# Replacing TensorE's spreading of the picks' first halves by a round trip through memory

## The reference

```python
# 8 heads x 16 picks = 128 experts per token, out of 128 x 128 experts;
# expert = 128 * first_half + second_half, each half in 0..127
hid  = hn . down[expert]                # per token and pick: one number
coef = gate * gelu(hid)
h   += sum over picks of coef * up[expert]
out  = rms_norm(h, final_norm_gain)
```

## Time and profile before

| what | value |
|---|---|
| median of 3 runs | 2948.95 us |
| lowest, highest | 2944.47, 2950.55 us |
| the profiled execution's own time | 2950.64 us |
| its span | 2948.8 us |
| TensorE busy | 2814.4 us (95%) |
| VectorE busy | 2062.5 us (70%) |
| ScalarE busy | 1118.8 us (38%) |
| GpSimd busy | 539.3 us (18%) |
| moved | 799.60 MB, 271 GB/s on the mean |

### The profile page before, as it was taken

The page is one execution under the profiler, slowest core; times in us unless marked ns, Lnnn a source line. Parts: engine busy times, 40 slices in busy tenths (PEclk is TensorE's granted clock), DMA queues, the critical chain, the costliest instruction groups (busy, mean ns, idle before and its releaser), DMA issues.

```text
span 2948.8 us, 41367 instructions
## 1 busy us (share of the span) xinstructions
PE 2814.4 (95%) x16385; PEld 2303.8 (78%) x16385; DVE 2062.5 (70%) x3111; ACT 1118.8 (38%) x1741; POOL 539.3 (18%) x534
## 2 busy tenths in 40 slices
PE   6899999999999999999999999999999889999997
PEld 4699999997879988798997798888878777444443
DVE  5687777778775456754655668985568999666666
ACT  3344444445454444544455542012117986000000
POOL 1000000000000000000000002333445457544443
PEclk9999999999999999999999999999999999999999
DMA  9977777777866644365443546999998888999997
GB/s 386 351 261 265 265 267 263 267 266 252 299 207 189 175 124 156 127 200 176 136 123 128 198 140 234 349 331 391 403 366 282 291 295 317 407 409 409 409 410 319
DMA packets 345760, 799.60 MB, mean 271 GB/s; under 512 B 40104, under 2 KB 95648, under 8 KB 344800
## 3 DMA queue, kind: packets, MB, share of 16 engines
q1 hardware_dynamic: 270576, 505.70, 49.6%
q0 software_dynamic: 74992, 291.27, 26.3%
HBM read 794.76 MB, written 2.10 MB: 270 GB/s over the span
## 4 chain that ended last, share of the span: by engine, by line
PE 53%; DMA 22%; DVE 13%; ACT 5%; issue 4%; POOL 3%; SPq 0%; DVEq 0%; ACTq 0%; POOLq 0%
PE ps L2019 16%; PE ps L2021 15%; PE ps L2020 15%; DMA s<-in_up_rows,s 12%; DMA s<-in_down_rows,s 8%; DVE s L1953 4%; POOL s L719 3%; DVE s L1972 2%; ACT s L1163 1%; DMA s<-in_ada_first 1%; DVE r L1246 1%; DMA s<-in_ret_first 1%; ACT r L734 1%; PE ps L2313 1%; ACT s L1133 1%
## 5 line engine op out<-in xcount | busy, mean ns | idle before, releaser
L2019 PE MATMUL ps<-r,r 128*128 128x256 f32 (+1 forms) x3232 | 1043.8, 323 | 9.9 <-DVE r L1246 7.6
L2021 PE MATMUL ps<-r,r 128*128 128x256 f32 (+1 forms) x3232 | 1024.2, 317 | 0.0
L2020 PE MATMUL ps<-r,r 128*128 128x256 f32 (+1 forms) x3232 | 1024.1, 317 | 0.0
L1246 DVE TENSOR_TENSOR r<-s,r 128x1024 fp32r<-128x1024 f32 (+2 forms) x532 | 640.3, 1212 | 413.1 <-ACT r L734 412.1
L734 ACT CAST r<-s 128x1024 fp32r<-128x1024 f32 (+2 forms) x532 | 550.0, 1041 | 766.7 <-PE ps L2021 708.2
L2019 PEld LDWEIGHTS ps<-r,r 128*128 128x128 f32 x3232 | 618.3, 191 | 67.0 <-issue 19.9
L2020 PEld LDWEIGHTS ps<-r,r 128*128 128x128 f32 x3232 | 618.6, 191 | 43.1 <-issue 5.3
L2021 PEld LDWEIGHTS ps<-r,r 128*128 128x128 f32 x3232 | 618.0, 191 | 40.2
L2703 PE MATMUL ps<-s,big 128*128 128x512 f32 x1024 | 441.8, 594 | 2.0 <-DMA s<-in_up_blocks 2.0
L1972 DVE SCALAR_TENSOR_TENSOR s<-s,s,s 128x1024 f32<-128x1024 f32 x256 | 329.2, 1286 | 162.9 <-DMA s<-in_up_rows,s 155.6
L1953 DVE CUSTOM_DVE_ANT_0 s<-s,s 128x1152 f32<-128x1152 f32 x256 | 345.8, 1353 | 111.2 <-DMA s<-in_down_rows,s 110.9
(11 more groups left out here) (314 smaller groups left out, 2240.4 us busy)
## 6 DMA issues: line engine op xcount, KB each, us to landing
s<-in_ada_w SPq DMA_DIRECT2D x128, 512.0 KB, 5.4
s<-in_up_blocks SPq DMA_DIRECT2D x128, 512.0 KB
s<-in_ret_w_in SPq DMA_DIRECT2D x112, 512.0 KB, 5.5
s<-in_down_blocks SPq DMA_DIRECT2D x128, 448.0 KB
s<-in_w_in SPq DMA_DIRECT2D x96, 512.0 KB, 3.9
s<-in_ada_first SPq DMA_DIRECT2D x64, 512.0 KB, 7.9
s<-in_ret_w_out SPq DMA_DIRECT2D x64, 512.0 KB, 5.6
s<-in_ret_w_in SPq DMA_DIRECT2D x112, 256.0 KB, 3.8
```

Source lines behind the costliest of these rows:

```text
L1246: v.tensor_tensor(lo_of(w), raw_of(w), hi_of(w).bitcast(F), ALU.subtract).then_inc(*lo_made.to(w))
L2019: pe.matmul(o, lh, rh, start=start, stop=False, skip_group_check=True)
L2020: pe.matmul(o, lh, rl, start=False, stop=False, skip_group_check=True)
L2021: return pe.matmul(o, ll, rh, start=False, stop=stop, skip_group_check=True)
```

## The change

The first halves of the picks no longer go through TensorE. SyncE stores them to a small tensor in memory (`first_halves`), in eight pieces, once they are chosen. During the picks it loads them back, one load of 256 KB for each group of four tokens, in which one row of 2 KB is repeated over the 128 partitions, into three buffers `FH`. VectorE's `pick` compares these with `POS` and reads the picked rows straight from PSUM, so that ScalarE's copy goes away.

Three things move with it. `FH` lies in the room of the streamed blocks, so SyncE stands in its loop of 64 loads until tile 1's picks are multiplied, and `up`'s blocks 128 and 129 come after that. Four single-use semaphores (`d_fg`, `d_tab`, `d_ff`, `d_f2`) become one, `d_late`. For that, the load of `final_norm_gain_2` is moved from SyncE's queue to GpSimd's: it is issued just before row 326.

```diff
+        FH = [at(W + 6144 + 512 * i, 512) for i in range(3)]
...
-        d_fg, d_tab, d_ff, d_f2, d_step = (dma_sig(n) for n in ("d_fg", "d_tab", "d_ff", "d_f2", "d_step"))
+        d_late, d_step = dma_sig("d_late", ["fg", "tab", "ff", "f2"]), dma_sig("d_step")
...
-        rows_copied = sig("rows_copied", fours)
+        d_kept = dma_sig("d_kept", [(t, k) for t in range(2) for k in range(4)])
+        d_halves = [dma_sig(f"d_halves{i}", [n for n in range(64) if n % 3 == i]) for i in range(3)]
...
             for b in range(256):
+                if b in (50, 82):
+                    t = b // 82
+                    sp.wait_ge(*chosen.at((t, 1)))
+                    for k in range(4):
+                        sp.dma_start(A["halves"][t].rearrange("(q k) m -> k q m", k=4)[k],
+                                     EF[t][32 * k:32 * k + 32, 0, :]).then_inc(*d_kept.to((t, k)))
+                if b == 128:
+                    sp.wait_ge(*d_kept.at((1, 3)))
+                    sp.wait_ge(*block_used.at(127))
+                    for n in range(64):
+                        if n >= 3:
+                            sp.wait_ge(*multiplied.at(fours[n - 3]))
+                        sp.dma_start(FH[n % 3], A["halves"][n // 32].rearrange("(q k) m -> q (k m)", k=4)[n % 32].partition_broadcast(
+                            128)).then_inc(*d_halves[n % 3].to(n))
+                    sp.wait_ge(*multiplied.at((1, 31)))
...
-                if b == 128:
-                    sp.wait_ge(*block_used.at(127))
...
-                if b == 131:
-                    sp.dma_start(G16[0:16, :], A["final_norm_gain_2"].rearrange("(n p) -> n p", p=128)).then_inc(*d_f2.to("all"))
...
                 if n == RINGS[3][0] + 6:
                     g.wait_ge(*built.at((1, 31)))
+                    g.dma_start(G16[0:16, :], A["final_norm_gain_2"].rearrange("(n p) -> n p", p=128)).then_inc(*d_late.to("f2"))
...
-            def rows_copy(t, q):
-                s.wait_ge(*rows_picked.at((t, q)))
-                if 32 * t + q >= 3:
-                    s.wait_ge(*picked.at(fours[32 * t + q - 3]))
-                s.copy(PR[(32 * t + q) % 3], bank[3 + q % 2]).then_inc(*rows_copied.to((t, q)))
...
-                v.wait_ge(*rows_copied.at((t, q)))
-                v.scalar_tensor_tensor(out=o, in0=bank[first_half_bank(t, q)], scalar=POS, in1=o, op0=ALU.is_equal,
+                n = 32 * t + q
+                if n >= 3:
+                    v.wait_ge(*picked.at(fours[n - 3]))
+                v.wait_ge(*rows_picked.at((t, q)))
+                v.wait_ge(*d_halves[n % 3].at(n))
+                v.scalar_tensor_tensor(out=o, in0=FH[n % 3], scalar=POS, in1=bank[3 + q % 2], op0=ALU.is_equal,
                                        op1=ALU.mult).then_inc(*multiplied.to((t, q)))
...
-                take(b1)
-                for k in range(4):
-                    r = pe.matmul(bank[b1][:, k * 128:(k + 1) * 128], IDR[:, token(q, k):token(q, k) + 1].broadcast_to([128, 128]),
-                                  EFR[t][:, 0, :], start=True, stop=True)
                 r.then_inc(*rows_picked.to((t, q)))
-                free[b1], free[b] = multiplied.at((t, q)), rows_copied.at((t, q))
+                free[b] = multiplied.at((t, q))
...
-            pe.wait_ge(*d_f2.at("all"))
+            pe.wait_ge(*d_late.at("f2"))
...
+    A["halves"] = nc.dram_tensor("first_halves", (2, 128, 128), F, kind="Internal").ap()
```

More of the change, by code:

```diff
@@ L604, in second_bank @@
             return 2 if t or q % 2 == 0 else 6
-        def first_half_bank(t, q):
-            return 1 if t or q % 2 else 0
         BANK_OF = {(x, p): 2 + p % 4 if x == "N0" else (6, 7, 0, 1)[p] if x == "C" else p for x, p in pairs}
@@ L700, in gpsimd @@
             g.wait_ge(*rotated.at(("M", 3)))
-            g.dma_start(GBA, A["final_norm_g"].partition_broadcast(128)).then_inc(*d_fg.to("all"))
+            g.dma_start(GBA, A["final_norm_g"].partition_broadcast(128)).then_inc(*d_late.to("fg"))
             g.wait_ge(*fin_scaled.at((3, 1)))
-            g.dma_start(GBA[:, 0:896], A["table"][:, K_DM:K_END]).then_inc(*d_tab.to("all"))
+            g.dma_start(GBA[:, 0:896], A["table"][:, K_DM:K_END]).then_inc(*d_late.to("tab"))
             g.wait_ge(*att_out.at(("L", 15)))
-            g.dma_start(FFG, A["ffn_norm_gain_2"][0][D1:].partition_broadcast(128)).then_inc(*d_ff.to("all"))
+            g.dma_start(FFG, A["ffn_norm_gain_2"][0][D1:].partition_broadcast(128)).then_inc(*d_late.to("ff"))
             g.dma_start(STEPN, A["table"][:, K_STEP:K_ALL]).then_inc(*d_step.to("all"))
@@ L1182, in scalar @@
                 pick_hot_(0, q)
-                if q:
-                    rows_copy(0, q - 1)
             for q in range(33):
@@ L1187, in scalar @@
                     pick_hot_(1, q)
-                rows_copy(*fours[31 + q])
                 if q == 1:
@@ L1354, in project_out @@
                             if n == 0:
-                                v.wait_ge(*d_fg.at("all"))
+                                v.wait_ge(*d_late.at("fg"))
                             v.tensor_tensor(XN[:, t, n * 512:(n + 1) * 512], X[:, t, n * 512:(n + 1) * 512],
@@ L1714, in vector @@
                 gate_side(i)
-            v.wait_ge(*d_tab.at("all"))
+            v.wait_ge(*d_late.at("tab"))
             def dil_groups():
@@ L1811, in vector @@
                 turn("E", p, colA[:, 64:80], None, HT)
-            v.wait_ge(*d_ff.at("all"))
+            v.wait_ge(*d_late.at("ff"))
             v.wait_ge(*turn_lo.at(("E", 7)))
@@ L2603, in pick_rows @@
             def pick_rows(t, q):
-                b, b1 = 3 + q % 2, first_half_bank(t, q)
+                b = 3 + q % 2
                 take(b)
@@ L2608, in pick_rows @@
                 for k in range(4):
-                    pe.matmul(bank[b][:, k * 128:(k + 1) * 128], DH[:, 128 * t + token(q, k), :], PH[q % 2][:, k, :],
-                              start=True, stop=True)
-                take(b1)
-                for k in range(4):
-                    r = pe.matmul(bank[b1][:, k * 128:(k + 1) * 128], IDR[:, token(q, k):token(q, k) + 1].broadcast_to([128, 128]),
-                                  EFR[t][:, 0, :], start=True, stop=True)
+                    r = pe.matmul(bank[b][:, k * 128:(k + 1) * 128], DH[:, 128 * t + token(q, k), :], PH[q % 2][:, k, :],
+                                  start=True, stop=True)
                 r.then_inc(*rows_picked.to((t, q)))
-                free[b1], free[b] = multiplied.at((t, q)), rows_copied.at((t, q))
+                free[b] = multiplied.at((t, q))
             def add_picked(t, q):
```

## The result

The changed kernel takes **3012.85 us** (median of 4 runs, 3009.24 to 3015.14), against 2948.51 for the kernel before (4 runs): ratio **1.0216, 95% interval 1.0201 to 1.0230**, 64 us slower. Its profiled execution has a span of 3011.3 us, 62.5 more than before.

The account below looks back on a forecast made before the run. VectorE and its rows were taken to bound the picks, and TensorE dense `up`, with no slack for a late start. The sum +3 + 57 - 2 - 7 = +51 us on 2948.95 gave 3000 us, range 2984 to 3020.

Parts of the forecast that it names:

- The size of that delay: Start of dense `up`: TensorE waits for the final gain's load in GpSimd's queue and starts 57 us late (50 to 62).
- The landing of the gain: Before dense `up`: issued at 2532 us behind three rows of 0.5 MB, the 8 KB gain lands at about 2538.
- What comes back: Dense `up` and the tail: waits for blocks go and the end after the last matmul shortens, -2 and -7 us.
- +3 us for VectorE's shift: Picks of both tiles: the last row of `down` comes 3 us later (from 10 earlier to 18 later).
- 6 gained: Picks: VectorE's idle time removed by dropping the copy and TensorE's spreading, up to 8 us, taken as 6.
- 9 lost: Picks: added loads slow `down`'s rows; between 4 and 22 us, taken as 9.
- a row's landing: Picks: time from a row's issue to landing, set by added traffic between 5.70 us and 7.36 beside dense `down`.
- The upper value of 22: Picks: loss of 22 us if stalls add to the 2.13 us per row instead of replacing: 39 x 0.27 + 66 x 0.17.
- `FH` is late: Rival, tile 0's picks: first-halves loads landing in 10.8 us cost 44 us more, 3041 us in all; 6%.
- The rows are starved: Rival, picks: all 105 rows go at 2.33 us, 27 us in place of 3, 3024 us in all; 9%.
- The picks pay: Rival, picks: VectorE loses all 19 us of idle time, 2978 us in all; 5%.
- not slower: Rival, dense `up`: the gain's load goes out by 2480 us, so the start is prompt and only +3 stays, 2952; 2%.

Follow-up runs that it names:

- gain_moved: Kernel before the change, with only the final gain's load moved to GpSimd's queue ahead of row 326: 2996.55 us, ratio 1.0168.
- three_loads: Changed kernel with the gain's load back on SyncE's queue and three loads of first halves instead of 64: 2945.07 us, ratio 0.9984.
- gain_back: Changed kernel with only the final gain's load put back on SyncE's queue, behind block 131: 2966.35 us, ratio 1.0059.
- quarter_loads: Changed kernel, gain's load back on SyncE's queue, each first-halves load from the fourth on cut to 64 KB (512-byte pieces): 2961.74 us, ratio 1.0038.
- traffic_beside: Kernel before the change, with 64 loads of 256 KB added that nobody reads and blocks 128 and 129 behind them: 2973.28 us, ratio 1.0091.

## Why the prediction was right, point by point

- **Sign and main cause: right, and shown.** The forecast was 3000 us, in a range of 2984 to 3020; 3012.85 lies in it. (By the terms named the lower end is 2949 + 50 - 10 - 9 = 2980.) The gain's load behind row 325 holds TensorE, and dense `up` passes the delay on. gain_moved alone gives 50 us, with 57.2 - 9.7 = 47.5 expected.
- **The size of that delay: right to the microsecond, partly by luck.** Foreseen were 57 us over VectorE's own shift; measured 57.2. Its terms: from the 33rd row to the gain's issue 52.2 us (foreseen 50.4), from there to the small matmuls 4.4 (6), the small matmuls 7.1 (7). Two errors of nearly 2 us cancel. The granted clock was 0.50 during these matmuls, the level of 1.2 GHz, after a stand of 54.95 us; in the kernel before it had been 0.95 (2484 to 2488 us). They took 7.16 us where they had taken 3.93.
- **The landing of the gain.** I expected it behind row 325, itself 6.8 us after its issue. VectorE began on row 325 at 2552.9 at the latest, so that row took 5.9 us or less, and the gain landed at 2553.0, 4.3 us after its own issue. Whether the rows in front held it up at all is not shown. The load of 65 KB that I took to be alone on the queue (4.8 us) was not: it was issued at 1633.30, 0.5 us behind the load of 576 KB.
- **What comes back: right.** -1.9 and -7.8 us, with -2 and -7 foreseen.
- **The term that was mis-sized: the picks.** I took +3 us for VectorE's shift, made of 6 gained and 9 lost; it was 15.0 (2.0 of them ahead of the picks, within what the runs of one kernel differ by). The gain side held where the loads are left out: some 5 us by three_loads. The loss side did not: the loads cost 22 us by the pair of gain_back and three_loads. Two steps made it too small.
- **First, a row's landing was put between two values by the traffic added**: 6.8 us in tile 0 and 6.4 in tile 1. Measured in gain_back were 7.1 and 6.9 (medians), the same 1.2 us over three_loads in both tiles though tile 1 has fewer loads per us; and a quarter of the bytes slowed the rows nearly as much. In this case a landing did not go with the traffic added. For 66 rows of tile 1 in four buffers, 0.5 us are 8 us.
- **Second, the 6 us gained were taken off once more.** With these landings four buffers allow (7.1 + 1.9) / 4 = 2.25 us per row in tile 0 and 2.20 in tile 1, slower than the 2.13 and 2.04 that the forecast starts from: 39 x 0.12 + 66 x 0.16 = 15 us. Once the buffers set the pace, VectorE's other waits are no longer there to be won. This estimate meets the 13.0 us of the picks in the profile and the 17 of gain_back. Over the pace of three_loads (2.03 and 2.00 us per row from the first pick on) it gives 22 us. So slower landings can have replaced the other stalls, as the forecast had it, and still have cost this much; VectorE's waits for rows (16.0 to 34.7 us) would grow either way and don't decide it. The upper value of 22 in the forecast met the number, but by adding 0.27 and 0.17 us to each row, and no run shows that working.
- **Small errors of the working.** Until 2287.4 us tile 0 has 40 rows and not 39 (the 41 of the earlier trace rows count one that began before): 2.08 us per row and not 2.13. The pace beside dense `down` is 2.31 in one place and 2.33 in another. The 5.70 us for a row among the picks was the shortest of the four such steps in the chain of waits from 2205 us on (7.04, 5.70, 7.01, 6.39); the medians of three_loads (5.7) and of gain_moved (5.6), with its picks as before, bear it out all the same.
- **The rivals.** *`FH` is late* is out: 3.7 to 6.6 us of waits in all. But it came near: the forecast had a load land in 3.5 us, from rows of GpSimd's queue (and the estimate of 2.6 quoted beside it is further off), where on SyncE's queue the median was 6.2, close to the 6.6 at which it decides. *The rows are starved* came near for the picks: 22 us, where it said 27. *The picks pay* and *not slower* are out for this kernel.

## What to carry to other kernels

A small load that is moved to another queue costs the wait for its place there, not its bytes: write down what stands ahead of it, who waits for it, and whether the stage behind is full, for then each microsecond goes through to the end. In a stage that lives on gathers in few buffers, streams added on another queue can cost by what they do to the gathers' landing, even where bandwidth is left (quarter_loads, 288 GB/s) and the new loads are never waited for (traffic_beside). Work out the pace that the buffers allow at the later landing; if it is slower than the present one, what the change saves elsewhere does not come on top. And if work is taken off engines that do not bind, look first for the buffer that does: here a fifth buffer for the rows made both the old and the new picks faster.

## What the runs showed of the hardware that was not expected

- A quarter of the added bytes (64 KB a load in pieces of 512 bytes, 7.8% of the engines' time) cost 5.4 thousandths of the time, the whole (23.1%) 7.5, and 64 loads of 1 KB nothing.
- Half the bytes in half as many pieces cost as much as in all of them, within the intervals (1.0036 and 1.0041).
- Beside loads of 256 KB on SyncE's queue, a gathered row of 576 KB landed in 7.0 us and not 5.7 (medians of 90 and 101 rows in gain_back and three_loads).
- A load of 256 KB on SyncE's queue took 6.2 us to land beside the rows (median of gain_back).
- An 8 KB load issued 1.7 us behind a gathered row of 512 KB on the same queue landed in 4.3 us; that row landed within 5.9 us of its issue. Whether the one held up the other is not shown.
